# Two score steps of each softmax attention placed ahead of the last gate tile

## The reference

```
even:  q,k,v,f, q_r,k_r,v_r, z = split(rms_norm(x) @ w_in)
       c = cumsum(log_sigmoid(f + b_f))
       fox = softmax_causal(q k^T / 8 + c_i - c_j) @ v            # 8 heads of 64
       y = concat(fox, group_norm(retention(q_r, k_r, v_r))) * silu(z)
odd:   q, kc,vc, ks,vs, kw,vw, gl, z = split(rms_norm(x) @ w_in)
       o = g0 * softmax(q k_cmp^T ...) v_cmp                      # 31 compressed blocks
         + g1 * softmax_causal(q ks^T ...) vs + g2 * softmax_causal(q kw^T ...) vw   # 16 heads, 4 groups
       y = o * silu(z)
```

## Time and profile before

| | us |
|---|---|
| median of 3 runs | 1566.89 |
| lowest, highest | 1564.44, 1569.54 |
| the profiled execution | 1566.48 |
| its span | 1564.7 |
| mean granted TensorE clock | 0.981 |

### The profile page before, as it was taken

One profiled execution on the slowest core, in us unless ns is written; L12 is line 12 of the kernel. 1 busy time (PEld: TensorE's weight loads), 2 busy tenths in 40 slices (PEclk: granted clock), 3 DMA queues, 4 the chain that ended last, 5 costly groups with the idle time before them and its releaser, 6 DMA issues.

```text
span 1564.7 us, 24980 instructions
## 1 busy us (share of the span) xinstructions
PE 1476.0 (94%) x10148; PEld 947.0 (61%) x10148; DVE 973.4 (62%) x1946; ACT 882.0 (56%) x1247; POOL 67.6 (4%) x148
## 2 busy tenths in 40 slices
PE   6999998999989999999998999989699999899997
PEld 3444485665458448585787666445385755466676
DVE  6732547888478566555667224576756336699974
ACT  4544456777554665454553453657354557678862
POOL 0000000000100100000010000001000000000000
PEclk8999999999999999999999999999899999999999
DMA  6233232111422334433325366411023332200002
GB/s 183 87 102 108 87 103 81 55 55 54 156 86 82 129 108 122 119 112 108 108 87 76 97 91 96 94 54 32 21 88 105 117 108 81 81 1 2 2 12 85
DMA packets 127218, 132.07 MB, mean 84 GB/s; under 512 B 9760, under 2 KB 124192, under 8 KB 126976
## 3 DMA queue, kind: packets, MB, share of 16 engines
q1 hardware_dynamic: 124336, 119.59, 27.0%
q0 software_dynamic: 2768, 10.89, 2.0%
HBM read 128.38 MB, written 2.10 MB: 83 GB/s over the span
## 4 chain that ended last, share of the span: by engine, by line
PE 59%; DVE 8%; ACT 4%; issue 2%; DMA 2%; POOL 0%; ACTq 0%; DVEq 0%
PE bank L709 8%; PE bank L710 8%; PE bank L711 8%; PE bank L748 6%; PE bank L750 5%; PE bank L749 5%; PE bank L942 3%; PE bank L924 3%; PE bank L915 2%; DVE wring L1872 2%; PE bank L911 1%; ACT whigh L1274 1%; DMA wring<-in_even_w_in 1%; PE bank L824 1%; DVE scr L2399 1%
## 5 line engine op out<-in xcount | busy, mean ns | idle before, releaser
L709 PE MATMUL bank<-xT,whigh 128*128 128x512 f16 x960 | 366.1, 381 | 10.4 <-DVE xT L2045 7.7
L710 PE MATMUL bank<-xT,whigh 128*128 128x512 f16 x960 | 366.0, 381 | 0.0
L711 PE MATMUL bank<-xT,wring 128*128 128x512 f16 x960 | 365.6, 381 | 0.0
L1872 DVE SCALAR_TENSOR_TENSOR wring<-wring,wsc,whigh 128x2048 f16<-128x2048 f32 x105 | 245.0, 2334 | 165.6 <-ACT whigh L1274 165.1
L1274 ACT ACTIVATE whigh<-wring,wsc 128x2048 f16<-128x2048 f32 x105 | 208.8, 1988 | 156.4 <-DVE wsc L1775 138.0
L1291 ACT ACTIVATE whigh<-wring 128x2048 bf16<-128x2048 f32 x105 | 199.0, 1895 | 121.3 <-DMA wring<-in_even_w_in 43.5
L748 PE MATMUL bank<-whigh,slab 128*128 128x256 f16 x800 | 218.0, 273 | 3.0 <-DVE wring L1872 1.2
L750 PE MATMUL bank<-whigh,slab 128*128 128x256 f16 x800 | 218.1, 273 | 0.0
L749 PE MATMUL bank<-wring,slab 128*128 128x256 f16 x800 | 218.0, 273 | 0.0
L709 PEld LDWEIGHTS bank<-xT,whigh 128*128 128x128 f16 x960 | 94.4, 98 | 126.3 <-DVE xT L2045 7.9
L711 PEld LDWEIGHTS bank<-xT,wring 128*128 128x128 f16 x960 | 94.4, 98 | 114.7 <-issue 2.5
(11 more groups left out here) (324 smaller groups left out, 2356.3 us busy)
## 6 DMA issues: line engine op xcount, KB each, us to landing
wring<-in_w_in SPq DMA_DIRECT2D x28, 1024.0 KB, 5.1
wring<-in_w_up SPq DMA_DIRECT2D x16, 1024.0 KB, 5.3
wring<-in_w_down SPq DMA_DIRECT2D x16, 1024.0 KB, 5.2
wring<-in_even_w_in SPq DMA_DIRECT2D x14, 1024.0 KB, 9.5
wring<-in_odd_w_in SPq DMA_DIRECT2D x14, 1024.0 KB, 4.9
wring<-in_w_a SPq DMA_DIRECT2D x4, 1024.0 KB, 5.2
wring<-in_w_out SPq DMA_DIRECT2D x4, 1024.0 KB, 5.2
wring<-in_even_w_out SPq DMA_DIRECT2D x4, 1024.0 KB, 4.7
```

The source lines that it names most:

```text
L709: pe.matmul(bank, wh[:, k, wcol:wcol + width], xh[:, k, :], start=k == 0, stop=False)
L710: pe.matmul(bank, wh[:, k, wcol:wcol + width], xl[:, k, :], start=False, stop=False)
L711: mm = pe.matmul(bank, wl[:, k, wcol:wcol + width], xh[:, k, :], start=False, stop=k == KC - 1)
L1872: dve.scalar_tensor_tensor(low_of(i)[:, :, 0:m], loaded(i)[:, :, 0:m], wsc[:, n:n + 1], high_of(i)[:, :, 0:m], ALU.mult, ALU.subtract).the ...
```

## The change

Each attention function takes the iterations to run. `EARLY`, iterations 0 and 1, is called ahead of gate tile 7 on TensorE and behind gate tile 6 on ScalarE and VectorE; `later`, from 2 on, follows all gates. TensorE now waits for six read gate tiles ahead of the first scores, and for all eight only ahead of the first transposes (i == 3); in the odd layer it waits for the copies of the compressed attention at the first values (i == 4). The even gates move to `ZBANKS`, with a wait for the retention values' banks ahead of tile 2, the sigmoids to scratch rows 4 and 5. `gated_scale` goes from iteration 2 to 6. The sigmoid counts of three stages share a semaphore.

```diff
--- before
+++ after
@@ counted semaphores @@
+        sigmoid_made = sem("sigmoid_made")
+        for i, stage in enumerate(("q", "ze", "zo")):
+            counted[stage + "_sg"] = sigmoid_made, 8 * i
@@ class Att @@
                 self.steps = [(m, b, parts) for m in range(heads // 2) for b in range(branches) for parts in TILES]
+                self.later = range(2, len(self.steps) + 8)
...
+        EARLY = range(2)
@@ TensorE: attention @@
-            def attention(A):
+            def attention(A, some):
...
-                for i in range(N + VALUE_LAG):
+                for i in some:
...
                         mm.then_inc(s_(n + "_sc"), 1)
+                    if i == TURN_LAG:
+                        gate = {"fox": "ze_ev", "nsa": "zo_ev"}[n]
+                        pe.wait_ge(s_(gate), n_(gate, 8))
+                    if i == VALUE_LAG and n == "nsa":
+                        pe.wait_ge(s_("ct_ev"), 16)
...
-                    if i >= VALUE_LAG:
+                    if VALUE_LAG <= i < N + VALUE_LAG:
@@ TensorE: even layer @@
-            feat("ze", 8, xhalves, SA)
-            pe.wait_ge(s_("ze_ev"), n_("ze_ev", 8))
-            pe.wait_ge(s_("vr_ev"), n_("vr_ev", 8))
-            pe.wait_ge(s_("frow_both"), 1)
-            pe.wait_ge(s_("decay_in"), 32)
-            attention(FOX)
+
+            def fox_start():
+                pe.wait_ge(s_("ze_ev"), n_("ze_ev", 6))
+                pe.wait_ge(s_("frow_both"), 1)
+                pe.wait_ge(s_("decay_in"), 32)
+                attention(FOX, EARLY)
+
+            feat("ze", 8, xhalves, ZBANKS, before={2: lambda: pe.wait_ge(s_("vr_ev"), n_("vr_ev", 8)), 7: fox_start})
+            attention(FOX, FOX.later)
@@ TensorE: odd layer @@
-            feat("zo", 8, xhalves, ZBANKS, before={m: lambda m=m: between_gates(m) for m in range(1, 8)})
+
+            def nsa_start():
+                between_gates(7)
+                pe.wait_ge(s_("zo_ev"), n_("zo_ev", 6))
+                pe.wait_ge(s_("cs_ev"), 16)
+                pe.wait_ge(s_("ks_ev"), n_("ks_ev", 2))
...
+                attention(NSA, EARLY)
+
+            feat("zo", 8, xhalves, ZBANKS, before={7: nsa_start, **{m: lambda m=m: between_gates(m) for m in range(1, 7)}})
             compressed_turn(7)
-            pe.wait_ge(s_("cs_ev"), 16)
-            pe.wait_ge(s_("zo_ev"), n_("zo_ev", 8))
-            pe.wait_ge(s_("ct_ev"), 16)
...
-            attention(NSA)
+            attention(NSA, NSA.later)
@@ ScalarE (the even gate loop now stands behind the definition of attention) @@
-                act.activation(scr[:, m % 2, :], SA[m % 4][:, :], ACT.Sigmoid, scale=undo("ze", m // 2)).then_inc(s_("ze_sg"), 1)
+                act.activation(scr[:, 4 + m % 2, :], ZBANKS[m % 4][:, :], ACT.Sigmoid, scale=undo("ze", m // 2)).then_inc(s_("ze_sg"), 1)
                 act.wait_ge(s_("ze_sg"), own(s_("ze_sg")))
                 if m % 2 == 0:
                     following("ze", m // 2)
+                if m == 6:
+                    attention(FOX, EARLY)
 
             act.wait_ge(s_("ze_ev"), n_("ze_ev", 8))
-            attention(FOX)
+            attention(FOX, FOX.later)
...
-                act.activation(scr[:, m % 2, :], ZBANKS[m % 4][:, :], ACT.Sigmoid, scale=undo("zo", m // 2)).then_inc(s_("zo_sg"), 1)
+                act.activation(scr[:, 4 + m % 2, :], ZBANKS[m % 4][:, :], ACT.Sigmoid, scale=undo("zo", m // 2)).then_inc(s_("zo_sg"), 1)
...
+                if m == 6:
+                    attention(NSA, EARLY)
+            attention(NSA, NSA.later)
@@ VectorE @@
-                for i in range(max(lows) + 1):
-                    if i == 2:
+                for i in some:
+                    if i == 6:
                         gated_scale(name)
...
+            def behind_even_gate(m):
+
+                if m >= 1:
+                    bound_behind("ze", m - 1)
+                if m == 6:
+                    attention(FOX, EARLY)
+
+            silu("ze", slab[5], ZBANKS, {m: lambda m=m: behind_even_gate(m) for m in range(8)})
+            bound_behind("ze", 7)
...
                 if m >= 1:
                     bound_behind("zo", m - 1)
+                if m == 6:
+                    attention(NSA, EARLY)
```

More of the change, by code:

```diff
@@ L1188, in _ @@
             pe.wait_ge(s_("gl_ev"), n_("gl_ev", 1))
-            feat("zo", 8, xhalves, ZBANKS, before={m: lambda m=m: between_gates(m) for m in range(1, 8)})
-            compressed_turn(7)
-            pe.wait_ge(s_("cs_ev"), 16)
-            pe.wait_ge(s_("zo_ev"), n_("zo_ev", 8))
-            pe.wait_ge(s_("ct_ev"), 16)
[L1194 to L1197, removed]
-            attention(NSA)
+            def nsa_start():
[3 more added lines that the diff above has]
+                pe.wait_ge(s_("ks_ev"), n_("ks_ev", 2))
+                pe.wait_ge(s_("ks_half"), 2)
+                pe.wait_ge(s_("kw_ev"), n_("kw_ev", 2))
+                pe.wait_ge(s_("kw_half"), 2)
+                attention(NSA, EARLY)
+            feat("zo", 8, xhalves, ZBANKS, before={7: nsa_start, **{m: lambda m=m: between_gates(m) for m in range(1, 7)}})
+            compressed_turn(7)
+            attention(NSA, NSA.later)
             pe.wait_ge(*out_made("oo", 7))
@@ L1571, in attention @@
                 highs = {VALUE_LAG + per * (m + 1) + 1: m for m in range(pairs)}
-                for i in range(max(highs) + 1):
+                for i in some:
                     if i in highs:
@@ L1593, in attention @@
                         ins.then_inc(s_(n + "_ex"), 1)
+            for m in range(8):
+                if m % 2 == 0:
+                    period("ze", m // 2)
+                act.wait_ge(s_("ze_mm"), n_("ze_mm", m + 1))
+                if m >= 2:
+                    act.wait_ge(s_("ze_ev"), n_("ze_ev", m - 1))
+                act.activation(scr[:, 4 + m % 2, :], ZBANKS[m % 4][:, :], ACT.Sigmoid, scale=undo("ze", m // 2)).then_inc(s_("ze_sg"), 1)
+                act.wait_ge(s_("ze_sg"), own(s_("ze_sg")))
+                if m % 2 == 0:
+                    following("ze", m // 2)
+                if m == 6:
+                    attention(FOX, EARLY)
             act.wait_ge(s_("ze_ev"), n_("ze_ev", 8))
-            attention(FOX)
+            attention(FOX, FOX.later)
             def ret_copies(m):
@@ L2325, in silu @@
                     dve.wait_ge(s_(name + "_sg"), n_(name + "_sg", m + 1))
-                    dve.scalar_tensor_tensor(dst[:, m, :], banks[m % 4][:, :], undo(name, m // 2), scr[:, m % 2, :], ALU.mult,
+                    dve.scalar_tensor_tensor(dst[:, m, :], banks[m % 4][:, :], undo(name, m // 2), scr[:, 4 + m % 2, :], ALU.mult,
                                              ALU.mult).then_inc(s_(name + "_ev"), 1)
@@ L2339, in bound_behind, with attention @@
                 gate_bound(name, slab[5], row)
-            silu("ze", slab[5], SA, {m: lambda m=m: bound_behind("ze", m - 1) for m in range(1, 8)})
-            bound_behind("ze", 7)
-            def attention(A):
+            def attention(A, some):
                 n, steps, N = A.name, A.steps, len(A.steps)
```

## The result

The changed kernel takes 1570.74 us (median of 20 runs, 1568.36 to 1572.88), the kernel before 1567.01 us (20 runs, 1563.90 to 1569.54). The ratio is 1.0025, 95% interval 1.0019 to 1.0031: 3.9 us longer (3.0 to 4.9). The forecast was 1569.7, +3.2 us on the profiled execution. The profiled execution after took 1569.57 us, 3.1 more than that of before.

What follows compares the result with a forecast made beforehand. TensorE, busy 94%, was taken as the bound, its string from step 4 released by ScalarE's exponentials. Gains −1.18 and −0.23 plus clock losses 2.3 and 2.3 gave +3.2 on 1566.48: 1569.7 us, range 1563.5 to 1573.5.

Steps and rivals of the forecast that it cites:

- Where the end is set: Both attentions: TensorE has no gap from step 4 on, so the end moves with the start of step 4's scores.
- Scores moved: Even layer: scores of steps 0 and 1 go ahead of gate tile 7, which ends 3.28 us later.
- Early load hidden, the other two on the chain: ScalarE, each attention: three 1.28 us table loads; first under the masks' wait, those for tile 7's sigmoid and step-2 exponentials exposed.
- Odd layer: Start of step 4's scores in the odd attention: 1375.04 in place of 1375.27, a gain of 0.23 us, ScalarE late.
- `gated_scale`: Its 1.47 us on VectorE move from step 2 to step 6, into slack: 0, bounds 0 and 1.47 us per attention.
- The clock: TensorE idles over 5 us before step 4, then runs at half clock: 2.3 us lost per attention, bounds 0 and 3.1.
- The clock staying up: Rival: no half-clock work behind step 4's start in either attention, only the gains left, −1.4 us, 1565.1; chance 0.16.
- The loads on the chain: Rival: ScalarE's early table load comes behind the masks, early exponentials end 1.28 us later; +5.3 us, 1571.8; chance 0.22.
- The waits did not go: Rival denied here: TensorE loses all 11.25 us of idle ahead of step 4 in both layers; 1555.2; chance 0.12.
- The rule of the Trainium skill: ScalarE: finish one table set's work before switching; about 2.7 us per switch, 2.8 us more per attention than the trace's price.

Runs made afterwards that it cites:

- the fill: The changed kernel plus 16 (even) and 20 (odd layer) small unneeded TensorE matmuls behind the first transposes; 1564.76 us, ratio 0.9980 to the kernel before.
- e2_odd_only: The changed kernel with early steps in the odd layer only, the even attention run whole behind its gates, gated_scale there at step 2; 1572.71 us, ratio 1.0033.

## Why the prediction was right, step by step

- *Where the end is set.* Right. TensorE's string from step 4 on carries the start's shift to the attention's end: wherever the clock was full, the string kept its length to 0.02 us (34.87 or 34.88 even; 135.72 or 135.73 odd, 136.08 to 136.10 with `gated_scale` at step 6), with starts from 17.30 to 19.62 and 14.72 to 18.55.
- *Scores moved.* 3.28 us were forecast for tile 7's delay. Its last matmul starts 8.07 us behind tile 6's sigmoid (1032.03), 4.76 before (1026.75): 3.31.
- *Early load hidden, the other two on the chain.* Right for the first (no releaser, no delay) and the third (behind the minima). Half wrong for the sigmoid's: in the even layer it began at 1031.90, ahead of tile 7's last matmul (1032.03), so it did not wait for the tile as two waits had let me think. That gave the even layer the 0.5 us it gained beyond the forecast: 1.68 in place of 1.18.
- *Odd layer.* Forecast 0.23 us of gain, measured 0.24. ScalarE is the late one: its last early exponential ends just ahead of 1363.91, and tile 7 was long done.
- *`gated_scale`.* Taken at 0 in the steady steps. It is 0 in the even layer (34.88 with it at step 6 and a full clock). In the odd layer it is 0.35 us: 136.08 to 136.10 in the four profiles with it there and a full clock in the string, against 135.73. The bound was 0 to 1.47.
- *The clock.* Right in mechanism in the main, sizes off in opposite ways: 1.5 us in the even layer for 2.3, and 4.1 in the odd (140.19 − 136.09), beyond the bound of 3.1. The term that was mis-sized is the slow stretch in the odd string: 9.2 us long, where the rows it was taken from had 4.9 and 4.4, both of them projection work. And in the odd layer the joined idle piece was not what first brought the clock down: it had fallen in the kernel before too, and now fell some 1.6 us into the piece. What the change did there was to put the slow stretch into the string, and to lengthen it. Errors of −0.8 and +1.8 stand beside +0.35 and −0.5 of the other terms; the sum of +3.2 came out at +4.06 by the distances and +3.9 by the runs. That it came so close is in part luck: errors of up to 1.8 us in the terms left 0.9 us in their sum.
- *Rivals.* The clock staying up was made real by the fill and went as priced (−1.4 forecast, −1.6 by the distances; −3.1 timed, with −1.4 at the very edge of its interval). The loads on the chain did not come for the early one. The waits did not go: TensorE's idle pieces were joined, not removed, and in the odd layer two short ones stayed beside the long one (1.36 and 1.53 us).
- *The rule of the Trainium skill* on grouping functions by table set (ScalarE: Activation LUTs, "Table sets: the hidden batching unit"). The runs go the way it says: with one switch per attention in place of three, and the clock held up in both kernels, the start is sooner, 14.72 for 18.13 us in the odd layer and 17.30 for 17.93 in the even. The order of the exponentials changed with it, so not all of this is the loads. Each load takes 1.28 us here, and the next activation starts 1.30 us behind its start (1031.90 to 1033.20). The measured length decides, not the 2.7 us that the Trainium skill gives for a switch.

## What to carry to other kernels

A wait of the busiest engine is worth only what the last chain behind it gives back. Work out the next moment at which that engine is released, with all that the helpers do in order; here 11.25 us of idle gave 1.9 us of earlier starts in the order that was tried first, and 6.0 in the best. And ask what shape the idle takes: two short waits joined into one of over 5 us let TensorE's clock fall in the even layer, and in both layers the slow work then lay where nothing covered it. Where a wait can't be shortened, TensorE can be kept busy with matmuls into a free bank, but that pays only if what follows is on the chain; and functions of two table sets should not be interleaved for a gain that another order gives without it.

## What the runs showed of the hardware

- Half-clock stretches behind an idle piece of 5 to 6 us lasted 3 to 5 us of gapless work in the even attention and 8.5 to 9.2 us in the odd one, in four profiles out of four. With 8.12 us of idle ahead, and the same TensorE work, it was 3.2 and 3.7 us in the odd one. The cause is open.
- The wait of 3.49 us ahead of step 2's scores in the even layer kept clock 1.00 in the profile before. It was followed by a mean of 0.59 and 0.60 over the next 4.2 us with `gated_scale` moved alone and in `e2_odd_only`: the same order of work on TensorE, another outcome.
- A table load for an activation can start ahead of the activation's wait (1359.71, with the activation released later by VectorE), also where the code has two waits there (1031.90, ahead of tile 7's last matmul at 1032.03). At 1038.83 the load came behind its wait. What decides was not found.
- A float32 matmul of 128 by 128 by 128 added 0.23 us to TensorE's queue (32 records in 3.74 us for 16 of them), and with them in the idle piece the clock stayed at 1.00.
